# Sparse attention on one core: a deeper ring of steps, two passes over the heads, and top-k selections moved to other places

## The chip, the cores and the metric

The kernel runs on one NeuronCore of a Trainium2 chip. The metric is the device time of one execution in microseconds (us), as the median of several executions. Matrix products run on TensorE (PE in the rows, PEld for its weight loads), the elementwise work on VectorE (DVE) and ScalarE (ACT), some additions on GpSimd (POOL); SyncE (SP) issues the DMAs.

## The reference, cut to what matters

A block of several layers over 528 tokens (16 meta tokens and 512 real ones), of width 1024, all in fp32. The change touches only the sparse attention of the second layer, with 16 heads over a shared latent of rank 256:

```python
def _dsa_attention(h, pos, cid, w_in, latent_norm, w_uq, q_norm, w_uv, rel_bias, k_sel):
    ...
    q_abs, q_idx = jnp.split(c_q @ w_uq, [B_HEADS * B_KV_RANK], axis=-1)
    q_abs = _rms_norm(q_abs.reshape(bsz, t, B_HEADS, B_KV_RANK), q_norm)
    ...
    def block(qa, qi, wi, qpos):
        act = jax.nn.relu(jnp.einsum("bqhd,bsd->bqhs", qi, k_idx) * IDX_DIM ** -0.5)
        score = jnp.einsum("bqh,bqhs->bqs", wi, act).astype(jnp.float32)
        score = jnp.where(cid[None, :] <= cid_q[:, None], score, NEG_INF)
        _, sel = lax.top_k(score, k_sel)            # k_sel = 128
        ...
        logits = (jnp.einsum("bqhr,bqkr->bqhk", qa, kv).astype(jnp.float32) * B_KV_RANK ** -0.5
                  + jnp.swapaxes(bias, -1, -2))
        p = jax.nn.softmax(jnp.where(valid[:, :, None, :], logits, NEG_INF), axis=-1)
        o_lat = jnp.einsum("bqhk,bqkr->bqhr", p.astype(kv.dtype), kv)
        o = jnp.einsum("bqhr,hrd->bqhd", o_lat, w_uv)
```

Each query takes part with the 128 keys of highest index score only. The kernel computes the attention over all keys that a tile of queries can see, and adds a mask of -1e30 where a key is not among the 128.

## The kernel before, in words

Everything stands in `latent_heads`. The 512 queries are cut into four tiles of 128 (`REAL_TILES`); tile t sees 144, 272, 400 or 528 keys. The stage has three parts.

**The query part.** TensorE computes the absorbed queries of the 16 heads (`query`, L1500, four 128x512 products for a head), ScalarE squares them and copies them to `q_all` (L1601, L1603), GpSimd adds the squares and TensorE sums them (`sums`, L1507). Between the queries of heads 0 to 7 stand 40 index jobs, five to a head: a job is one index head of one tile, or half of one for tile 3 (`jobs`; widths 144, 272, 400 and 264). TensorE computes the score (L1516), ScalarE applies the relu (L1591), VectorE adds it into `mb` (L1654, L1657). When a tile's jobs are done, VectorE selects its 128 best keys at once: 16 times `max` and `match_replace` in a loop (L1664 to L1667), each pair taking eight values, then two instructions that turn the row into the mask (L1669, L1671). The engines are tied in a short ring: a relu waits for the addition two jobs back, an index score for the relu three jobs back. So a selection on VectorE holds ScalarE and then TensorE, queries too, since each engine's queue is in order.

**The attention part** runs 64 steps, (head, tile) with the tile running fastest. A step has: two score products on TensorE for each run of up to 512 keys (`scores`, L1535); on VectorE the scaled scores plus bias (L1689) and the mask and row maximum (L1692), together `logit`; on ScalarE the exponentials and their sum (`exps`, L1614); on VectorE the reciprocal of the sum and a diagonal matrix of it (`weigh`, L1698, L1700); on TensorE the transposes of the exponentials against that diagonal (`turn`, L1549); on ScalarE the copy out of the banks (`spread`, L1624, L1628); on TensorE the product with the values (`outputs`, L1559) and on ScalarE its copy (`store`, L1634). The order is written out by hand:

```python
for g in range(LAST):        # TensorE
    turn(g)
    if g + 2 < LAST:
        scores(g + 2)
    if g:
        outputs(g - 1)
for g in range(LAST):        # VectorE
    weigh(g)
    if g + 2 < LAST:
        logit(g + 2)
```

`turn(g)` waits for `weigh(g)`, and `logit(g + 2)` for `scores(g + 2)`. The scores of a step lie in two PSUM banks of their own, of four.

**The output product** (L1580) follows when the last head is stored.

Of the kernel before, what the change touches and what calls it, by code (L numbers as in the profile page):

```python
# [15 lines left out]
P = 128  # L16
# [41 lines left out]
def build(nc, x_t, meta_t, mem_t, bias_onehot, dil_onehot, rel_bias, dil_table, gains, wi, wo, w_out,  # L58
# [3 lines left out]
    with top:  # L62
# [1132 lines left out]
        def dsa_stage():  # L1195
            with ExitStack() as st:
# [8 lines left out]
                early = sb(st, "b_work", [P, 3648])  # L1205
# [225 lines left out]
        def latent_heads(st, qn, ckv, vals, g_lat, kidx, widx, qidx, eps_q, mb, mix, bw, c_bw, early, w_uq, uq_there):  # L1431

            q_all = sb(st, "l_q_all", [P, 2 * B_HEADS, SEQ])
# [4 lines left out]
            nmx = sb(st, "l_nmx", [P, 2])  # L1438
            den = sb(st, "l_den", [P, 2])
            rden = sb(st, "l_rden", [P, 2])  # L1440
# [5 lines left out]
            diag = early[:, 4 * TOK + 10 * P:4 * TOK + 12 * P].rearrange("p (s q) -> p s q", s=2)  # L1446
# [9 lines left out]
            flat = acc[:, :, :].rearrange("p b c -> p (b c)")  # L1456
# [13 lines left out]
            with nc.Block() as block:  # L1470
# [21 lines left out]
                def _(pe):  # L1492
# [36 lines left out]
                    def scores(g):  # L1529
                        hd, t = STEPS_[g]  # L1530
                        _, q0, keys, _ = REAL_TILES[t]
                        for a in range(0, keys, BANK):
                            b = min(keys, a + BANK)
                            for r in range(2):
                                last = pe.matmul(flat[:, 2 * BANK * (g % 2) + a:2 * BANK * (g % 2) + b],  # L1535
                                                 q_all[:, 2 * hd + r, q0 - META:q0 - META + P], ckv[:, r, a:b],
                                                 start=r == 0, stop=r == 1)
                        last.then_inc(scored, 1)

                    def turn(g):  # L1540
                        keys = REAL_TILES[g % NT][2]
# [3 lines left out]
                        for j, n in key_tiles(keys):  # L1545
                            if j == 4 and g >= 2:
                                pe.wait_ge(mixed, 1 + g - 1)
                            to = acc[0:n, 4 + g % 2, j * P:(j + 1) * P] if j < 4 else acc[0:n, 6 + g % 2, P:2 * P]
                            last = pe.matmul(to, e[:, g % 2, j * P:j * P + n], diag[:, g % 2, :], start=True, stop=True)  # L1549
# [14 lines left out]
                    scores(0)  # L1564
                    scores(1)
                    for g in range(LAST):
                        turn(g)
                        if g + 2 < LAST:
                            scores(g + 2)
                        if g:  # L1570
                            outputs(g - 1)
                    outputs(LAST - 1)
                    for c in range(KC):
# [3 lines left out]
                        for k in range(KC):  # L1577
                            if c == 0:
                                pe.wait_ge(mixed, 1 + 2 * NT * (k + 1))
# [5 lines left out]
                def _(act):  # L1585
# [25 lines left out]
                    def exps(g):  # L1611
                        keys = REAL_TILES[g % NT][2]
                        act.wait_ge(logits, 1 + g + 1)
                        act.activation(e[:, g % 2, 0:keys], lg[:, g % 2, 0:keys], ACT.Exp, scale=-1.0,  # L1614
                                       bias=nmx[:, g % 2:g % 2 + 1], accum_out=den[:, g % 2:g % 2 + 1]
                                       ).then_inc(expd, 1)

                    def spread(g):
                        keys = REAL_TILES[g % NT][2]
# [17 lines left out]
                    exps(0)  # L1637
                    exps(1)
                    for g in range(LAST):
# [3 lines left out]
                        if g + 2 < LAST:  # L1643
                            exps(g + 2)
# [3 lines left out]
                def _(dve):  # L1648
                    for n, (i, hd, a, b) in enumerate(jobs):
                        keys = META + (i + 1) * P  # L1650
                        score = mb[:, i, 0:keys]
# [8 lines left out]
                        if hd < IDX_HEADS - 1 or b < keys:  # L1660
                            continue
                        dve.memset(mb[0:CHUNK, i, keys - CHUNK:keys], MASKED)
# [6 lines left out]
                        dve.tensor_scalar(score, score, TAKEN / 1.5, MASKED, ALU.is_gt, ALU.mult)  # L1669
                        dve.drain()  # L1670
                        dve.memset(mb[0:CHUNK, i, keys - CHUNK:keys], MASKED)  # L1671
                        dve.drain()
# [11 lines left out]
                    def logit(g):  # L1684
                        hd, t = STEPS_[g]
                        _, _, keys, y0 = REAL_TILES[t]
                        s = g % 2
# [7 lines left out]
                    def weigh(g):  # L1695
                        s = g % 2
# [5 lines left out]

                    logit(0)
                    logit(1)
                    for g in range(LAST):
                        weigh(g)
                        if g + 2 < LAST:
                            logit(g + 2)
# [1238 lines left out]
```

## Time and profile before

| | us |
|---|---|
| runs | 4040.41, 4052.23, 4040.86 |
| median | 4040.86 |
| the profiled execution's own time | 4044.16 |
| its span in the profile | 4042.5 |
| TensorE busy in the span | 3721.5 (92%) |
| VectorE busy in the span | 1703.9 (42%) |
| query part, first index score to first attention score | 1680.3 to 1841.3 |
| attention part, first score to first output product | 1841.3 to 2122.1 |

A busy TensorE is not TensorE at its peak: the granted clock has two levels, 1.00 (2.4 GHz) and 0.50 (1.2 GHz), and its mean over the span is 0.961. The chain of waits in this profile covers no part of the stage, so the stage is read from its timeline, its waits and its windows.

### The profile page before, as it was taken

To read this page: it belongs to the slowest core of one execution; us is meant where nothing else is said; L and a number is where in the kernel's file an instruction comes from. 1 tells how busy PE (TensorE), PEld (TensorE's weight loads), DVE (VectorE), ACT (ScalarE), POOL (GpSimd) and SP (SyncE) were. 2 spreads that over 40 slices of the span, in tenths; PEclk is the share of its full clock that TensorE was granted. 3 is DMA by queue.
4 is the path that set the end of the run, shared out by engine and by line. 5 is a ranking of instruction groups with operands and counts; after the bars stand their busy time and mean duration, and the time that the engine had idled before them with its cause. 6 is when DMAs were issued, how large, how long until landed. Compare 5 with 4: busy or idle time off the path is not lost. (4 is left out here: it accounts for less than half of the span.)

```text
span 4042.5 us, 51723 instructions
## 1 busy us (share of the span) xinstructions
PE 3721.5 (92%) x20512; PEld 2965.1 (73%) x20512; DVE 1703.9 (42%) x2607; ACT 1277.1 (32%) x1796; POOL 301.0 (7%) x247
## 2 busy tenths in 40 slices
PE   8999798799999998768889999999889899899997
PEld 7999676699999997435555888888634377447886
DVE  4442377344334432253333443443258633225432
ACT  4331466233223321123332432342110143104321
POOL 0000222000000000010000000000045232000000
PEclk9999899799999999879999999999989999999999
DMA  4322311022222223000002222222212231223221
GB/s 166 131 77 79 112 53 48 32 94 88 80 99 89 90 79 126 8 21 16 1 1 94 93 94 93 104 93 88 99 39 78 89 96 53 101 75 114 94 85 71
DMA packets 115307, 318.04 MB, mean 79 GB/s; under 512 B 13335, under 2 KB 56471, under 8 KB 99060
## 3 DMA queue, kind: packets, MB, share of 16 engines
q1 hardware_dynamic: 115188, 316.48, 22.8%
q8 instruction: 71, 1.16, 0.1%
q14 instruction: 48, 0.39, 0.0%
HBM read 307.95 MB, written 17.01 MB: 80 GB/s over the span
## 5 line engine op out<-in xcount | busy, mean ns | idle before, releaser
L326 PE MATMUL acc<-fb_xh,fb_wh 128*128 128x264 f32 x1408 | 287.9, 286 | 11.7 <-DVE fb_wl L476 11.7
L326 PE MATMUL acc<-fb_xl,fb_wh 128*128 128x264 f32 x1408 | 288.3, 286 | 0.0
L326 PE MATMUL acc<-fb_xh,fb_wl 128*128 128x264 f32 x1408 | 287.7, 286 | 0.0
L326 PE MATMUL acc<-fd_xh,fd_wh 128*128 128x512 f32 x704 | 275.4, 391 | 9.6 <-DVE fd_wl L476 9.6
L326 PE MATMUL acc<-fd_xl,fd_wh 128*128 128x512 f32 x704 | 274.4, 390 | 0.0
L326 PE MATMUL acc<-fd_xh,fd_wl 128*128 128x512 f32 x704 | 274.4, 390 | 0.0
L326 PEld LDWEIGHTS acc<-fb_xh,fb_wh 128*128 128x128 f32 x1408 | 220.1, 189 | 12.1 <-DVE fb_wl L476 11.9
L326 PEld LDWEIGHTS acc<-fb_xl,fb_wh 128*128 128x128 f32 x1408 | 219.4, 189 | 0.0
L326 PEld LDWEIGHTS acc<-fb_xh,fb_wl 128*128 128x128 f32 x1408 | 219.1, 189 | 0.0
L397 ACT ACTIVATE fb_wh<-fb_raw 128x2048 fp32r<-128x2048 f32 (+1 forms) x74 | 124.7, 1685 | 290.1 <-PE acc L385 177.0
L471 DVE TENSOR_TENSOR fb_wl<-fb_raw,fb_wh 128x2048 fp32r<-128x2048 f32 (+1 forms) x74 | 148.3, 2004 | 141.4 <-ACT fb_wh L397 140.5
L471 DVE TENSOR_TENSOR fd_wl<-fd_raw,fd_wh 128x2048 fp32r<-128x2048 f32 (+1 forms) x74 | 148.3, 2003 | 136.5 <-ACT fd_wh L397 135.5
L397 ACT ACTIVATE fd_wh<-fd_raw 128x2048 fp32r<-128x2048 f32 (+1 forms) x74 | 124.8, 1686 | 255.8 <-PE acc L385 162.4
L397 ACT ACT_TABLE_LOAD x60 | 77.0, 1283 | 301.2 <-PE acc L326 301.1
L1874 PE MATMUL acc<-m_xn,s_gw 128*128 128x512 f32 x384 | 171.5, 603 | 0.0
L326 PEld LDWEIGHTS acc<-fd_xh,fd_wh 128*128 128x128 f32 x704 | 132.5, 188 | 38.5 <-DVE fd_wl L476 10.7
L326 PE MATMUL acc<-fa_xh,fa_wh 128*128 128x264 f32 x704 | 144.3, 286 | 11.9 <-DVE fa_wl L476 11.9
L326 PEld LDWEIGHTS acc<-fd_xl,fd_wh 128*128 128x128 f32 x704 | 132.5, 188 | 27.9 <-issue 0.5
L326 PEld LDWEIGHTS acc<-fd_xh,fd_wl 128*128 128x128 f32 x704 | 132.4, 188 | 27.5
L326 PE MATMUL acc<-ff_xh,ff_wh 128*128 128x512 f32 x352 | 138.2, 393 | 8.0 <-DVE ff_wl L476 8.0
L1874 PEld LDWEIGHTS acc<-m_xn,s_gw 128*128 128x128 f32 x384 | 72.7, 192 | 98.2 <-issue 98.2
L326 PE MATMUL acc<-fa_xl,fa_wh 128*128 128x264 f32 x704 | 144.5, 287 | 0.0
(523 smaller groups left out, 8472.2 us busy)
## 6 DMA issues: line engine op xcount, KB each, us to landing
fb_raw<-wi_dram SPq DMA_DIRECT2D x42, 1024.0 KB, 4.7
fd_raw<-wi_dram SPq DMA_DIRECT2D x42, 1024.0 KB, 4.7
fb_raw<-wo_dram SPq DMA_DIRECT2D x32, 704.0 KB, 3.9
fd_raw<-wo_dram SPq DMA_DIRECT2D x32, 704.0 KB, 4.0
fa_raw<-wi_dram SPq DMA_DIRECT2D x20, 1024.0 KB, 4.7
ff_raw<-wi_dram SPq DMA_DIRECT2D x20, 1024.0 KB, 4.7
a_raw<-a_qkv_dram SPq DMA_DIRECT2D x24, 512.0 KB, 4.0
s_gw<-gate_w_dram SPq DMA_DIRECT2D x24, 512.0 KB, 3.9
```

The source lines that it names most:

```text
L326: last = pe.matmul(acc[:, up_base(p, b) + 2 * a + q, 0:w], x[:, k, a, :], part[:, k, t0:t0 + w], start=k == 0 and part is xh and x is wv, ...
L397: act.activation(wh[:, b, 0:n_], raw[:, b, 0:n_], ACT.Copy).then_inc(rounded, 1)
L471: dve.tensor_tensor(wl[:, b, 0:n_], raw[:, b, 0:n_], wh[:, b, 0:n_].bitcast(F32), ALU.subtract).then_inc(split, 1)
L1874: last = pe.matmul(acc[:, GATE_BANK[n % 2], :], gw[:, n % 3, k * P:(k + 1) * P], xn[:, k, :], start=k == 0, stop=k == KC - 1)
```

## The change

What it does:

- The steps run in two passes over the heads: first tiles 0 and 1 of all 16 heads, then tiles 2 and 3.
- Four steps are in flight in place of two (`DEEP`), each with one score bank, and `scores`, `logit` and `exps` run three steps ahead (`AHEAD`). The last 16 keys of tile 3 don't fit into its bank; their scores are computed with those of tile 2, in whose bank they find room, and VectorE reads them by an instruction of its own. The exponentials are written over the logits.
- The selection of tile 0 is spread between the index jobs of tiles 1 to 3: one `pick` (a `max` and a `match_replace`) after every second job. Those of tiles 1 and 2 come in one piece each after the last job. That of tile 3 moves into the first pass: one `pick` after the `logit` at tile 1 of heads 0 to 13, two at heads 6 and 13.

```diff
+            DEEP, AHEAD = 4, 3
...
-            lg = early[:, 0:2 * TOK].rearrange("p (s t) -> p s t", s=2)
-            e = early[:, 2 * TOK:4 * TOK].rearrange("p (s t) -> p s t", s=2)
+            lg = early[:, 0:4 * TOK].rearrange("p (s t) -> p s t", s=DEEP)
...
-            STEPS_ = [(hd, t) for hd in range(B_HEADS) for t in range(NT)]
+            STEPS_ = [(hd, t) for first in (0, 2) for hd in range(B_HEADS) for t in (first, first + 1)]
+            REST_AT = REAL_TILES[NT - 2][2]
...
                     def scores(g):
                         hd, t = STEPS_[g]
-                        for a in range(0, keys, BANK):
-                            b = min(keys, a + BANK)
+                        if g >= DEEP:
+                            pe.wait_ge(logits, 1 + g - DEEP + (2 if t == NT - 2 else 1))
+
+                        def part(to, t_, a, b):
+                            q0 = REAL_TILES[t_][1] - META
                             for r in range(2):
-                                last = pe.matmul(flat[:, 2 * BANK * (g % 2) + a:2 * BANK * (g % 2) + b],
-                                                 q_all[:, 2 * hd + r, q0 - META:q0 - META + P], ckv[:, r, a:b],
-                                                 start=r == 0, stop=r == 1)
+                                last = pe.matmul(acc[:, g % DEEP, to:to + b - a], q_all[:, 2 * hd + r, q0:q0 + P],
+                                                 ckv[:, r, a:b], start=r == 0, stop=r == 1)
+                            return last
+
+                        last = part(0, t, 0, min(REAL_TILES[t][2], BANK))
+                        if t == NT - 2:
+                            last = part(REST_AT, NT - 1, BANK, TOK)
                         last.then_inc(scored, 1)
...
-                    scores(0)
-                    scores(1)
+                    for g in range(AHEAD):
+                        scores(g)
                     for g in range(LAST):
                         turn(g)
-                        if g + 2 < LAST:
-                            scores(g + 2)
+                        if g + AHEAD < LAST:
+                            scores(g + AHEAD)
                         if g:
                             outputs(g - 1)
...
+                    def pick(i):
+                        score = mb[:, i, 0:META + (i + 1) * P]
+                        dve.max(top8[:, :], score)
+                        dve.drain()
+                        dve.match_replace(out=score, in_to_replace=top8[:, :], in_values=score, imm_value=TAKEN)
+                        dve.drain()
...
                     for n, (i, hd, a, b) in enumerate(jobs):
...
-                        with dve.Fori(0, TOPK // 8):
-                            dve.max(top8[:, :], score)
-                            dve.drain()
-                            dve.match_replace(out=score, in_to_replace=top8[:, :], in_values=score, imm_value=TAKEN)
-                            dve.drain()
...
+                        done = n + 1 - IDX_HEADS
+                        if done > 0:
+                            rest = len(jobs) - IDX_HEADS
+                            for _ in range(done * PICKS // rest - (done - 1) * PICKS // rest):
+                                pick(0)
+                    visible(0)
+                    for i in (1, 2):
+                        with dve.Fori(0, PICKS):
+                            pick(i)
+                        visible(i)
...
                     def logit(g):
...
-                        dve.scalar_tensor_tensor(lg[:, s, 0:keys], flat[:, 2 * BANK * s:2 * BANK * s + keys],
-                                                 rq[:, t, hd:hd + 1], bw[:, hd, y0:y0 + keys], ALU.mult, ALU.add)
+                        own = min(keys, BANK)
+                        dve.scalar_tensor_tensor(lg[:, s, 0:own], acc[:, s, 0:own], rq[:, t, hd:hd + 1],
+                                                 bw[:, hd, y0:y0 + own], ALU.mult, ALU.add)
+                        if keys > BANK:
+                            dve.scalar_tensor_tensor(lg[:, s, BANK:keys], acc[:, s - 1, REST_AT:REST_AT + keys - BANK],
+                                                     rq[:, t, hd:hd + 1], bw[:, hd, y0 + BANK:y0 + keys],
+                                                     ALU.mult, ALU.add)
...
+                    LATE, LAST_PICK = NT - 1, B_HEADS - 3
                     for g in range(LAST):
+                        hd, t = STEPS_[g]
                         weigh(g)
-                        if g + 2 < LAST:
-                            logit(g + 2)
+                        if g + AHEAD < LAST:
+                            logit(g + AHEAD)
+                        if t == 1 and hd <= LAST_PICK:
+                            for _ in range((hd + 1) * PICKS // (LAST_PICK + 1) - hd * PICKS // (LAST_PICK + 1)):
+                                pick(LATE)
+                            if hd == LAST_PICK:
+                                visible(LATE)
```

`exps`, `turn` and `weigh` follow with `g % DEEP`, and `PICKS` is 16.

How this moves instructions, on VectorE first. In the query part, around the end of the jobs of tile 0 (`b_mb` holds the index scores and later the mask, `b_work` the relus), before:

```order
L1657 SCALAR_TENSOR_TENSOR b_mb<-b_work,b_widx,b_mb 128x144 x7
L1662 MEMSET b_mb 64x64
L1664 UNCONDITIONAL_BRANCH
L1665 MAX l_top<-b_mb 128x8
L1667 MATCH_REPLACE b_mb<-l_top,b_mb 128x144
L1664 REGISTER_ALU
L1664 COMPARE_AND_BRANCH
L1669 TENSOR_SCALAR b_mb<-b_mb 128x144
L1671 MEMSET b_mb 64x64
L1654 TENSOR_SCALAR b_mb<-b_work,b_widx 128x272
```

and in the changed kernel:

```order
L1681 SCALAR_TENSOR_TENSOR b_mb<-b_work,b_widx,b_mb 128x144 x7
L1685 MEMSET b_mb 64x64
L1678 TENSOR_SCALAR b_mb<-b_work,b_widx 128x272
L1681 SCALAR_TENSOR_TENSOR b_mb<-b_work,b_widx,b_mb 128x272
L1661 MAX l_top<-b_mb 128x8
L1663 MATCH_REPLACE b_mb<-l_top,b_mb 128x144
L1681 SCALAR_TENSOR_TENSOR b_mb<-b_work,b_widx,b_mb 128x272 x2
L1661 MAX l_top<-b_mb 128x8
L1663 MATCH_REPLACE b_mb<-l_top,b_mb 128x144
```

The loop of 16 rounds that stood ahead of the next tile's jobs is gone from there; its rounds stand one by one between those jobs.

In the attention part, VectorE over one step and a half, before (in `b_work` lie the logits and the diagonals here; the row ISA is the mask and maximum):

```order
L1689 SCALAR_TENSOR_TENSOR b_work<-acc,l_rq,b_bw 128x144
L1692 ISA b_work,l_nmx<-b_work,b_mb 128x144
L1692 ISA l_nmx 128x1
L1698 RECIPROCAL l_rden<-l_den 128x1
L1700 TENSOR_SCALAR b_work<-ident,l_rden 128x128
L1689 SCALAR_TENSOR_TENSOR b_work<-acc,l_rq,b_bw 128x272
```

and in the first pass of the changed kernel:

```order
L1714 SCALAR_TENSOR_TENSOR b_work<-acc,l_rq,b_bw 128x144
L1721 ISA b_work,l_nmx<-b_work,b_mb 128x144
L1721 ISA l_nmx 128x1
L1661 MAX l_top<-b_mb 128x8
L1663 MATCH_REPLACE b_mb<-l_top,b_mb 128x528
L1727 RECIPROCAL l_rden<-l_den 128x1
L1729 TENSOR_SCALAR b_work<-ident,l_rden 128x128
L1714 SCALAR_TENSOR_TENSOR b_work<-acc,l_rq,b_bw 128x272
```

A `pick` of tile 3, 528 wide, has come between a `logit` and the `weigh` that follows it; that `weigh` is of the step two before the `logit`'s, where it was one before.

In the second pass on VectorE:

```order
L1714 SCALAR_TENSOR_TENSOR b_work<-acc,l_rq,b_bw 128x512
L1717 SCALAR_TENSOR_TENSOR b_work<-acc,l_rq,b_bw 128x16
L1721 ISA b_work,l_nmx<-b_work,b_mb 128x528
L1721 ISA l_nmx 128x1
L1727 RECIPROCAL l_rden<-l_den 128x1
L1729 TENSOR_SCALAR b_work<-ident,l_rden 128x128
```

The row of 528 that stood at L1689 for tile 3 is now two rows, of 512 and 16.

## Rows read from the trace of the kernel before

**Rows 1.** Windows: us, then busy us of each engine, granted clock, DMA share, GB/s.

```profile
1680.30:1841.30 161.00, 104.92 (x336) 54.87 (x337) 90.71 (x244) 48.72 (x88) 20.33 (x16) 0.77 0.07 22
1855.30:2122.10 266.80, 223.91 (x1193) 140.08 (x1191) 89.08 (x307) 91.71 (x309) 0.00 (x0) 1.00 0.00 1
```

**Rows 2.** Waits over the query part: engine and line, waited for, us, times, longest.

```profile
PE acc L1516 <- ACT b_work L1591: 54.2, 7, 22.2
```

**Rows 3.** Timeline of the query part, TensorE and VectorE: start, us, operation, [idle before].

```profile
1700.31 0.72 PE L1516 MATMUL acc<-b_work 64*128 64x272 f32 x2
...
1721.30 0.11 DVE L1662 MEMSET b_mb<- 64x64 f32 x1
...
1743.84 0.43 DVE L1654 TENSOR_SCALAR b_mb<-b_work,b_widx 128x400 f32<-128x400 f32 x1
...
1755.81 0.11 DVE L1662 MEMSET b_mb<- 64x64 f32 x1
...
1782.68 0.81 DVE L1654 TENSOR_SCALAR b_mb<-b_work,b_widx 128x264 f32<-128x264 f32 x2
...
1794.81 1.15 PE L1516 MATMUL acc<-b_work 64*128 64x264 f32 x6
...
1801.98 1.16 PE L1516 MATMUL acc<-b_work 64*128 64x264 f32 x6
...
1806.37 0.11 DVE L1662 MEMSET b_mb<- 64x64 f32 x1
```

**Rows 4.** Timeline of VectorE, last selection, and the first logit.

```profile
1833.15 0.71 DVE L1665 MAX8 l_top<-b_mb 128x8 f32<-128x528 f32 x1 [0.34 <-issue]
...
1834.01 0.69 DVE L1667 MATCH_REPLACE8 b_mb<-l_top,b_mb 128x528 f32<-128x528 f32 x1
...
1841.49 0.23 DVE L1675 SCALAR_TENSOR_TENSOR l_mean_u<-acc,b_eps_q 128x64 f32<-128x64 f32 x1 [4.00 <-PE acc L1507]
...
1842.74 0.37 DVE L1689 SCALAR_TENSOR_TENSOR b_work<-acc,l_rq,b_bw 128x144 f32<-128x144 f32 x1
```

**Rows 5.** Timeline of TensorE over one head of the attention part.

```profile
1949.47 1.18 PE L1535 MATMUL acc<-b_ckv,l_q_all 128*128 128x272 f32 x4
...
1952.26 0.81 PE L1549 MATMUL acc<-b_work 128*128 128x128 f32 x4 [0.44 <-DVE b_work L1700]
1953.00 1.61 PE L1535 MATMUL acc<-b_ckv,l_q_all 128*128 128x400 f32 x4
...
1956.47 1.03 PE L1549 MATMUL acc<-b_work 128*128 128x128 f32 x6 [0.49 <-DVE b_work L1700]
1957.43 2.33 PE L1535 MATMUL acc<-b_ckv,l_q_all 128*128 128x512 f32 x8
...
1961.90 1.26 PE L1549 MATMUL acc<-b_work 128*128 128x128 f32 x8 [1.41 <-DVE b_work L1700]
1963.09 0.76 PE L1535 MATMUL acc<-b_ckv,l_q_all 128*128 128x144 f32 x4
...
1965.18 1.48 PE L1549 MATMUL acc<-b_work 128*128 128x128 f32 x10 [0.39 <-DVE b_work L1700]
```

**Rows 6.** Timeline of VectorE, a logit of the same head.

```profile
1963.88 0.37 DVE L1689 SCALAR_TENSOR_TENSOR b_work<-acc,l_rq,b_bw 128x144 f32<-128x144 f32 x1 [2.04 <-PE acc L1535]
```

**Rows 7.** Groups of instructions, VectorE at 16 elements out of PSUM: busy, mean ns, idle before.

```profile
L1063 DVE CUSTOM_DVE_ANT_0 a_lg<-acc,a_bw 128x16 f32<-128x16 f32 x16 | 2.1, 168 | 0.0
```

**Rows 8.** Timeline of TensorE at the half clock, start of the attention part.

```profile
1845.77 1.33 PE L1549 MATMUL acc<-b_work 128*128 128x128 f32 x4 [1.60 <-DVE b_work L1700]
1847.03 3.04 PE L1535 MATMUL acc<-b_ckv,l_q_all 128*128 128x400 f32 x4
```

**Rows 9.** Windows in two other stages (columns as in rows 1).

```profile
440.00:455.80 15.80, 8.40 (x31) 7.20 (x32) 9.44 (x12) 7.91 (x12) 7.60 (x6) 0.50 0.33 109
3439.00:3442.40 3.40, 3.40 (x10) 2.68 (x9) 0.36 (x1) 0.94 (x1) 0.00 (x0) 0.51 0.00 0
```

**Rows 10.** Timeline of TensorE ahead of the second of these windows.

```profile
3437.78 1.09 PE L2376 MATMUL acc<-ident,d_xe 128*128 128x128 f32 x8 [2.31 <-DVE d_xe L2642]
```

More of the change, by code:

```diff
@@ L1548, in turn @@
                             to = acc[0:n, 4 + g % 2, j * P:(j + 1) * P] if j < 4 else acc[0:n, 6 + g % 2, P:2 * P]
-                            last = pe.matmul(to, e[:, g % 2, j * P:j * P + n], diag[:, g % 2, :], start=True, stop=True)
+                            last = pe.matmul(to, lg[:, g % DEEP, j * P:j * P + n], diag[:, g % DEEP, :],
+                                             start=True, stop=True)
                         last.then_inc(turned, 1)
@@ L1635, in store @@
                                        acc[0:64, 6 + g % 2, 0:P], ACT.Copy).then_inc(mixed, 1)
-                    exps(0)
-                    exps(1)
+                    for g in range(AHEAD):
+                        exps(g)
                     for g in range(LAST):
@@ L1648, in _, with visible @@
                 def _(dve):
+                    PICKS = TOPK // 8
+                    def pick(i):
[4 more added lines that the diff above has]
+                        dve.drain()
+                    def visible(i):
+                        keys = META + (i + 1) * P
+                        dve.tensor_scalar(mb[:, i, 0:keys], mb[:, i, 0:keys], TAKEN / 1.5, MASKED, ALU.is_gt, ALU.mult)
+                        dve.drain()
+                        dve.memset(mb[0:CHUNK, i, keys - CHUNK:keys], MASKED)
+                        dve.drain()
                     for n, (i, hd, a, b) in enumerate(jobs):
                         keys = META + (i + 1) * P
-                        score = mb[:, i, 0:keys]
                         dve.wait_ge(relued, 1 + n + 1)
@@ L1659, in _ @@
                         dve.drain()
-                        if hd < IDX_HEADS - 1 or b < keys:
-                            continue
-                        dve.memset(mb[0:CHUNK, i, keys - CHUNK:keys], MASKED)
-                        dve.drain()
-                        with dve.Fori(0, TOPK // 8):
-                            dve.max(top8[:, :], score)
-                            dve.drain()
-                            dve.match_replace(out=score, in_to_replace=top8[:, :], in_values=score, imm_value=TAKEN)
-                            dve.drain()
[L1669 to L1672, printed above, removed]
+                        if hd == IDX_HEADS - 1 and b == keys:
+                            dve.memset(mb[0:CHUNK, i, keys - CHUNK:keys], MASKED)
+                            dve.drain()
+                        done = n + 1 - IDX_HEADS
[8 more added lines that the diff above has]
+                        visible(i)
                     dve.wait_ge(ssq_mm, 1 + B_HEADS)
@@ L1701, in weigh @@
                                           ALU.mult).then_inc(weights, 1)
-                    logit(0)
-                    logit(1)
+                    for g in range(AHEAD):
+                        logit(g)
+                    LATE, LAST_PICK = NT - 1, B_HEADS - 3
                     for g in range(LAST):
+                        hd, t = STEPS_[g]
                         weigh(g)
-                        if g + 2 < LAST:
-                            logit(g + 2)
+                        if g + AHEAD < LAST:
+                            logit(g + AHEAD)
[4 more added lines that the diff above has]
+                                visible(LATE)
                     for c in range(KC):
```

32 lines of the change are left out of this document (15 added, 17 removed).

## The prediction

> **What bounds the kernel now.** No chain of waits crosses the stage, so I read it from windows, waits and timelines. The windows [rows 1] part it in two. In the query part TensorE is busy for 104.9 of 161 us at a mean clock of 0.77; in the attention part for 224 of 267 us at 1.00. The reader should see that the first part idles and runs slow, the second hardly idles.
>
> In the query part TensorE's longest waits are at the index scores, 54.2 us in seven waits, the longest 22.2 [rows 2]. They stand where VectorE selects: 22.5 us between the memset at 1721.30 and the next tile's work at 1743.84, and 26.9 us from 1755.81 to 1782.68 [rows 3]. Where nothing is selected, a head with five jobs takes 7.17 us (1794.81 to 1801.98) [rows 3]. So VectorE's selections bound this part, by way of the in-order queues.
>
> In the attention part every `turn` is preceded by an idle time that a `weigh` ends: 0.44, 0.49, 1.41 and 0.39 us in a head, 2.73 together [rows 5]. VectorE in turn begins a `logit` right behind the scores, after waiting 2.04 us for them [rows 6]. That is a closed chain: turn(g), scores(g+2), logit(g+2), weigh(g+1), turn(g+1). `outputs` lies inside the VectorE leg and is hidden in all four steps.
>
> **Query part, step by step.** Both kernels do the same up to 1700.31, the end of the third query; the first selection had just begun. From there the new kernel has five more queries with jobs. At 7.17 us each that is 35.9, and the jobs of 400 keys add some 0.4 to each of two heads: 36.7, so the eighth query ends at about 1737.0. A `pick` of tile 0 is short, and two or three in a head fit beside the additions into 7.17 us, so I cost them at nothing; their cover is the query on TensorE. Behind the last query with jobs VectorE took 4.4 us before (1801.98 to 1806.37) [rows 3]; with two picks of tile 0 and the mask I take 6.8, to 1743.8. Then tiles 1 and 2 in one piece, 22.5 + 26.9 less 0.4 for the memsets that stand elsewhere: 49.0, to 1792.8. TensorE has the last eight queries beside this and is done some 17 us earlier, so its terms cost nothing. The first logit followed 1.25 us after L1675 [rows 4]; now at 1794.1, before at 1842.74. **Gain: 48.6 us.** Of this 31 is the selection of tile 3, which only moves; the rest is the stalls of tiles 0 to 2 at the full and half clock.
>
> **Attention part: does the depth remove a wait?** With three steps ahead the order is turn(g), scores(g+3), outputs(g-1) on TensorE and weigh(g), logit(g+3), weigh(g+1) on VectorE. `weigh(g+1)` still stands behind `logit(g+3)`, this behind `scores(g+3)`, and these behind `turn(g)`. The chain is the old one with another index. What becomes looser is the exponential, which was never waited for there. So I put the depth at zero. The order of tiles matters little too: every step is turn + scores + VectorE's leg, and each occurs as often as before. In pass one a pair of steps takes T0 0.74 (1952.26 to 1953.00), S1 with its leg 2.79 (1949.47 to 1952.26), T1 0.96 (1956.47 to 1957.43) and S0 with its leg 2.09 (1963.09 to 1965.18): 6.58 us [rows 5].
>
> - The picks of tile 3 stand between `logit(g+3)` and `weigh(g+1)`, on the chain, at steps where nothing else waits; no cover is left once `outputs` of 0.7 us is done. One is 0.86 from the start of MAX8 to that of MATCH_REPLACE8, 0.69 for the latter, and some 0.12 for the drain: 1.67 [rows 4] (the 0.34 "issue" is the loop's, which is gone). Sixteen are 26.7, the mask 0.8: **+27.5**.
> - Splitting the 528-wide logit adds an instruction of 16 elements from PSUM, on the chain sixteen times. The nearest row has 168 ns for such a one [rows 7]: **+2.7**.
> - The scores of the last 16 keys move from one step to its neighbour: 0. VectorE does three logits before the first `weigh` in place of two: **+0.6**. The new waits of `scores` are for logits three or four steps old: 0.
>
> At an unchanged clock this is +30.8, and the sum -17.8.
>
> **The clock.** Pass one gives TensorE less to do. A pair with a pick lasts 6.58 + 1.67 = 8.25 us, of which some 5.2 are busy, with an idle gap of about 2.4. It begins after 17 us of idleness, so at 0.50. Two rows speak of such a load. Between 440 and 456 TensorE worked in bursts, 8.4 of 15.8 us, and stayed at 0.50 all the time [rows 9]. At 3437.78 it came out of a gap of 2.31 us with short products only [rows 10], and the clock was 0.51 behind it, from 1.00 [rows 9]. In the attention part before the idle gaps were at most 1.41 and the clock held 1.00 [rows 1, 5]. So I expect pass one to run mostly at 1.2 GHz. Its price: T0 took 1.26 us there (1845.77 to 1847.03) against 0.74, a factor of 1.7 [rows 5, 8]; the products themselves can at most double. On T0 + T1 + S0 + S1 (0.74, 0.96, 0.76, 1.18) that is 2.5 to 3.0 us a pair, if VectorE's leg stays; in sixteen pairs 40 to 48. Before, the attention part paid about 4 for its own slow start, so 36 to 44, or 40, if the whole pass is slow. Since at the half clock a pair is one busy run of some 9 us, it may recover here and there; I take five sixths, **+33**. The bounds are 0 and +44.
>
> The Trainium skill (TensorE: Matmul & The Clock Gate, in the section Why this matters for your kernels) lays the drop of the clock to idle gaps longer than those worked out here. By that rule pass one would warm up and stay warm, and the sum would be -18. The trace speaks against it, since 2.31 us were enough at 3437.78; it stays as a rival below.
>
> **The sum:** -48.6 + 30.8 + 33 = +15, so 4059 against the profiled execution's own 4044.16. That execution lies 3.3 us above the median of the runs; **for the median I predict 4056 us.** A measurement of this kernel tells 0.3%, 12 us, from no change.
>
> **Rivals.**
>
> 1. *The clock recovers in about half of pass one.* For it: the unbroken runs of 9 us at the half clock. The term is 20 in place of 33: +2, 4043.
> 2. *The full clock through pass one*, as by the page's rule: -18, 4023. For it: 60% busy, no gap over 2.4. Against it: rows 9 and 10. This one ends on the faster side; it decides where the clock term is under 6.
> 3. *The jobs don't run freely.* The picks of tile 0 delay the additions, these the relus, and by the ring of three the queries, so that only the moved selection's 31 us come off: -31 + 31 + 33 = +33, 4074. For it: this ring made the stalls of rows 2. Against it: five additions and 2.5 picks need some 5.5 us of the 7.17.
> 4. *The depth does what it says*: VectorE runs ahead, the picks and the idle 2.73 us of a head are hidden. Then -48.6 - 44 + 3 = -90, 3951. Against it: the order above. The change not doing what it says is thus my forecast.
>
> **Chances.** Forecast 0.54, of which 0.18 falls within 12 us of no change and 0.36 above; its own range is 4047 to 4066. Rival 1 0.20, all within. Rival 2 0.14, 0.11 faster and 0.03 within. Rival 3 0.08, slower. Rival 4 0.04, faster. Faster 0.15, same 0.41, slower 0.44. The range takes in rival 2 at its lower end and all but the last of rival 3: 4023 to 4073; about 0.15 is left outside.
>
> **What would show it.** Right: first logit near 1794; TensorE without a long wait at the index scores; in pass one a pair of turns every 8 to 11 us, with a wait for L1729 of 2 us or more after each pick, and a granted clock near 0.5 over most of it; in pass two a wait ahead of each `turn` as before. Wrong: turns in pass one without these waits (rival 4), a clock of 1.00 there (rival 2), or index scores that wait for VectorE in the query part (rival 3).

## The result, and the profile after

| | before | changed kernel |
|---|---|---|
| median, us | 4046.14 (16 runs, 4040.41 to 4052.4) | 4053.46 (16 runs, 4047.74 to 4060.15) |
| the profiled execution, us | 4044.16 | 4050.23 |
| its span, mean granted clock | 4042.5, 0.961 | 4048.5, 0.956 |
| TensorE busy, us | 3721.5 | 3741.5 |
| VectorE busy, us | 1703.9 | 1709.2 |
| query part: first index score to L1675 / L1699 (`l_mean_u`), us | 161.2 | 117.1 |
| attention part: from there to the first output product, us | 280.6 | 332.3 |
| sum of both parts, us | 441.8 | 449.4 |

The ratio is 1.0018 with a 95% interval of 1.0010 to 1.0025: 7 us slower, less than the 0.3% that I called no change. The stage explains all of it: -44.1 us in its first part, +51.7 in its second, +7.6 together, where the two profiled executions are 6.1 us apart.

The windows of the changed kernel over the same stretches; the first answers to the query window of [rows 1], the other two are the first and the second pass, from the first `weigh` of a pass to the next pass, or to the last `weigh` (us, then busy us of each engine, granted clock, DMA share, GB/s):

```profile
1681.30:1798.40 117.10, 97.48 (x348) 53.08 (x348) 67.32 (x194) 48.76 (x88) 20.25 (x16) 0.89 0.12 39
...
1802.06:1964.65 162.59, 122.48 (x450) 71.05 (x450) 63.84 (x214) 40.57 (x160) 0.00 (x0) 0.72 0.00 1
1964.65:2121.98 157.33, 133.14 (x693) 83.71 (x694) 52.50 (x166) 50.56 (x147) 0.00 (x0) 0.99 0.00 1
```

The waits of the changed kernel in the stage, the engine and line, what it waited for, us, times, longest:

```profile
DVE b_work L1714 <- PE acc L1537: 189.1, 61, 5.2
PE acc L1555 <- DVE b_work L1729: 81.5, 52, 17.9
```

The same two waits in the kernel before:

```profile
DVE b_work L1689 <- PE acc L1535: 168.4, 63, 4.9
PE acc L1549 <- DVE b_work L1700: 46.4, 63, 1.9
```

The first says that VectorE still stands before nearly every `logit` waiting for the scores. The second says that TensorE still waits for `weigh` at most of the `turn`s. Four steps in flight have freed neither engine. Of the 54.2 us at the index scores [rows 2] 4.1 us are left, in six waits, the longest 1.8.

The query part, TensorE and VectorE (start, us, operation, [idle before]). It answers to [rows 3] and [rows 4]:

```profile
1721.72 3.70 PE L1500 MATMUL acc<-b_cq,b_w_uq 128*128 128x512 f32 x8
...
1729.06 5.40 PE L1500 MATMUL acc<-b_cq,b_w_uq 128*128 128x512 f32 x8
...
1737.92 3.70 PE L1500 MATMUL acc<-b_cq,b_w_uq 128*128 128x512 f32 x8
1741.55 1.16 PE L1516 MATMUL acc<-b_work 64*128 64x264 f32 x6
...
1748.58 0.45 DVE L1661 MAX8 l_top<-b_mb 128x8 f32<-128x272 f32 x1
...
1798.21 0.11 DVE L1671 MEMSET b_mb<- 64x64 f32 x1
...
1799.65 0.37 DVE L1714 SCALAR_TENSOR_TENSOR b_work<-acc,l_rq,b_bw 128x144 f32<-128x144 f32 x1
```

The eighth query ends at 1741.55, against the predicted 1737.0. One query of eight products took 5.40 us instead of 3.70, where the clock had fallen for a moment (the granted clock over the query is 0.68); the one at 1712.63 took 5.40 too. These two are 3.4 of the 4.5 us, and 0.9 is that the whole stage began that much later in this execution. The selections of tiles 1 and 2 then take 49.6 us (1748.58 to 1798.21; predicted 49.0).

A step with a pick in the first pass, at the full clock up to the turn and partly at the half clock behind it; it answers to [rows 5] and [rows 6]:

```profile
1879.28 0.37 DVE L1714 SCALAR_TENSOR_TENSOR b_work<-acc,l_rq,b_bw 128x144 f32<-128x144 f32 x1 [1.81 <-PE acc L1537]
...
1880.00 0.71 DVE L1661 MAX8 l_top<-b_mb 128x8 f32<-128x528 f32 x1
1880.78 0.09 DVE L1663 MATCH_VALUE_LOAD b_mb<-l_top,b_mb 128x8 f32 x1
1880.85 0.69 DVE L1663 MATCH_REPLACE8 b_mb<-l_top,b_mb 128x528 f32<-128x528 f32 x1
1881.62 0.16 DVE L1727 RECIPROCAL l_rden<-l_den 128x1 f32<-128x1 f32 x1
1881.86 0.28 DVE L1729 TENSOR_SCALAR b_work<-ident,l_rden 128x128 f32<-128x128 f32 x1
1882.20 0.81 PE L1555 MATMUL acc<-b_work 128*128 128x128 f32 x4 [2.24 <-DVE b_work L1729]
1882.94 1.70 PE L1537 MATMUL acc<-b_ckv,l_q_all 128*128 128x272 f32 x4
```

The chain of the prediction stands in these lines: scores, `logit`, the pick (1.62 us from 1880.00 to 1881.62), `weigh`, `turn`, with TensorE idle for 2.24 us at the end. At the two heads with two picks the gap is longer; the prediction, with "no gap over 2.4", had overlooked these. The first of them:

```profile
1872.79 1.02 PE L1555 MATMUL acc<-b_work 128*128 128x128 f32 x4 [3.87 <-DVE b_work L1729]
```

The clock can be read from the pairs of steps. Two such turns at the half clock, then two at the full clock:

```profile
1850.40 1.33 PE L1555 MATMUL acc<-b_work 128*128 128x128 f32 x4 [1.73 <-DVE b_work L1729]
...
1861.43 1.34 PE L1555 MATMUL acc<-b_work 128*128 128x128 f32 x4 [1.73 <-DVE b_work L1729]
...
1901.94 0.81 PE L1555 MATMUL acc<-b_work 128*128 128x128 f32 x4 [2.24 <-DVE b_work L1729]
...
1910.38 1.03 PE L1555 MATMUL acc<-b_work 128*128 128x128 f32 x4 [2.47 <-DVE b_work L1729]
```

11.03 us against 8.44: the half clock costs 2.6 us a pair, or 2.8 against the pair of 8.20 from 1823.40 to 1831.60, whose gaps are both 2.24; 2.5 to 3.0 were worked out. But the mean clock of the pass is 0.72, so it was at the lower level for 0.56 of the time (1 - 0.56 / 2 = 0.72), not for the five sixths that I took. Its first 16 us, from the first turn at 1802.64 on, are among that: TensorE had stood for 17.9 us ahead of it, as the selections of tiles 1 and 2 on VectorE end later than the last query.

### The profile page after: what moved, and what is told of

It reads as the page before. It is cut to its first block and busy times, and to the rows that moved or that the text cites. A ratio compares the mean times of both kernels' runs of the same rounds, so it can differ in the third digit from the quotient of the medians.

```text
span 4048.5 us, 51673 instructions
## 1 busy us (share of the span) xinstructions
PE 3741.5 (92%) x20512; PEld 2978.5 (74%) x20512; DVE 1709.2 (42%) x2623; ACT 1277.8 (32%) x1796; POOL 300.6 (7%) x247
## 5 line engine op out<-in xcount | busy, mean ns | idle before, releaser
L397 ACT ACTIVATE fd_wh<-fd_raw 128x2048 fp32r<-128x2048 f32 (+1 forms) x74 | 124.8, 1686 | 255.8 <-PE acc L385 162.4
L1555 PE MATMUL acc<-b_work 128*128 128x128 f32 (+1 forms) x448 | 82.6, 316 | 81.6 <-DVE b_work L1729 81.5
```

Of the source, the lines that this page charges most:

```text
L397: act.activation(wh[:, b, 0:n_], raw[:, b, 0:n_], ACT.Copy).then_inc(rounded, 1)
L1555: last = pe.matmul(to, lg[:, g % DEEP, j * P:j * P + n], diag[:, g % DEEP, :], start=True, stop=True)
```

## The experiments

The theory, in short: the attention part is a closed chain in which `weigh(g+1)` stands on VectorE behind `logit` of a later step; the depth does nothing because of that; the moved picks lengthen the chain by 1.6 us each; and with the idle gaps that they make the clock is lower. The rivals: the depth is worth or costs something by itself, the picks or the clock cost nothing, or another part of the change (order of tiles, split logit) makes the loss.

### One part of the change alone

**b3_attention_part**: the kernel before with the new attention part (four steps in flight, two passes, split logit), without any picks in it, and with the old query part. As a difference from the changed kernel:

```diff
-                        done = n + 1 - IDX_HEADS
-                        if done > 0:
-                            rest = len(jobs) - IDX_HEADS
-                            for _ in range(done * PICKS // rest - (done - 1) * PICKS // rest):
-                                pick(0)
-                    visible(0)
-                    for i in (1, 2):
-                        with dve.Fori(0, PICKS):
-                            pick(i)
-                        visible(i)
+                            with dve.Fori(0, PICKS):
+                                pick(i)
+                            visible(i)
...
-                        if t == 1 and hd <= LAST_PICK:
-                            for _ in range((hd + 1) * PICKS // (LAST_PICK + 1) - hd * PICKS // (LAST_PICK + 1)):
-                                pick(LATE)
-                            if hd == LAST_PICK:
-                                visible(LATE)
```

> The changed kernel with the query part of the kernel before (each tile selected at once behind its jobs), so the attention part alone: two passes, four steps in flight, the logit of 528 in two instructions, no picks in it. Theory (depth and order are worth nothing, the split 2.7 us and the start 0.6): 3 us more than before at an equal clock, 4047 to 4055 us. Rival 1 (the depth hides part of the wait ahead of turn): 4035 us or less. Rival 2 (the half clock comes of the short steps of the first pass, picks or not): 4060 us or more.

Measured: 4047.76 us, ratio 0.9998 (0.9989 to 1.0007). Its first pass and its wait ahead of the turns:

```profile
1847.64:1959.88 112.24, 89.83 (x450) 53.91 (x450) 39.55 (x162) 40.47 (x160) 0.00 (x0) 0.97 0.00 1
```

```profile
PE acc L1555 <- DVE b_work L1722: 48.2, 61, 1.6
```

The time is that of the kernel before, and inside the range expected. The depth, the passes and the split together cost 2.9 us in the attention part (283.5, before 280.6), about the 3.3 forecast for the split and the start; the wait ahead of the turns is 48.2 us, where it was 46.4. Against this kernel the changed one has 48.8 us more in its attention part (332.3 and 283.5). The picks are the only difference in the code there. Sixteen at 1.62 and the mask make 26.7. The remaining 22 I put down to the clock: the first pass ran at 0.97 without the picks, at 0.72 with them, though TensorE does the same work. They are a remainder, not a measurement, and hold the slow start behind the 17.9 us as well, which comes of the new query part and which this run doesn't have. A second estimate, from 0.56 of the pass in pairs of 11.03 us that each cost 2.6 to 2.8 more, gives 21 to 23.

**b2_query_part**: the kernel before with only the new query part, in which all four selections stay.

```diff
-                        if hd < IDX_HEADS - 1 or b < keys:
-                            continue
...
+                        done = n + 1 - IDX_HEADS
+                        if done > 0:
+                            rest = len(jobs) - IDX_HEADS
+                            for _ in range(done * PICKS // rest - (done - 1) * PICKS // rest):
+                                pick(0)
+                    visible(0)
+                    for i in (1, 2, 3):
+                        with dve.Fori(0, PICKS):
+                            pick(i)
+                        visible(i)
```

> The kernel before with only the query part changed: picks of tile 0 between the jobs, the selections of tiles 1, 2 and 3 in one piece behind the last job; the attention part as before. Theory (freeing the jobs is worth the stalls of TensorE, apart from the selection that moves): in the changed kernel the first logit came 118 us behind the first index score, and tile 3's selection adds 31, so 149.5 in place of 162.4: 13 us less, 4033 us, at most 4038. Rival (VectorE's total work sets the query part and only moving work away shortens it): 4046 us, no change.

Measured: 4036.91 us, ratio 0.9975 (0.9964 to 0.9987), within the expectation. The query part takes 150.8 us, 10.4 less than before and 33.7 more than in the changed kernel. These two can't be taken as they stand, since in this execution the clock was low for longer at the start of the part. The third query, here and in the changed kernel:

```profile
1697.38 3.70 PE L1500 MATMUL acc<-b_cq,b_w_uq 128*128 128x512 f32 x8
...
1697.60 3.70 PE L1500 MATMUL acc<-b_cq,b_w_uq 128*128 128x512 f32 x8
```

It begins 19.0 us behind the first index score (1678.39) here and 16.3 behind it (1681.26) there; before it was 16.4. The two queries ahead of it took 6.46 and 4.95 us here, 5.40 and 3.70 there. Without these 2.7 us the part is 148.1. So of the 44 us 31 are the last tile's selection, which only moves, as predicted, and 13 are the stalls, where the prediction had 17.6.

### The order on VectorE

**a1_pick_early**: the changed kernel with the pick ahead of the `logit`, where VectorE waits for the scores.

```diff
                         weigh(g)
-                        if g + AHEAD < LAST:
-                            logit(g + AHEAD)
                         if t == 1 and hd <= LAST_PICK:
...
+                        if g + AHEAD < LAST:
+                            logit(g + AHEAD)
```

> The changed kernel with each pick of tile 3 moved from behind logit(g+3) to ahead of it, that is into the time in which VectorE waits for the scores. Theory (the picks cost because they stand on the chain scores, logit, weigh, turn): VectorE waits 2 to 3.5 us there and a pick takes 1.67, so the 27 us of picks go, and with the shorter gaps on TensorE part of the half clock too, 10 to 21 us: 4006 to 4017 us. Rival (VectorE's work in the first pass is too much wherever it stands): 4045 us or more, no change by over 8.

Measured: 4018.92 us, ratio 0.9919 (0.9903 to 0.9936), 2 us above what the theory gave and far from the rival; the attention part takes 297.1 us, 35 less than in the changed kernel. From its timeline:

```profile
1873.22 0.70 DVE L1661 MAX8 l_top<-b_mb 128x8 f32<-128x528 f32 x1
...
1874.07 0.69 DVE L1663 MATCH_REPLACE8 b_mb<-l_top,b_mb 128x528 f32<-128x528 f32 x1
...
1875.12 0.37 DVE L1714 SCALAR_TENSOR_TENSOR b_work<-acc,l_rq,b_bw 128x144 f32<-128x144 f32 x1 [0.35 <-PE acc L1537]
...
1876.41 0.81 PE L1555 MATMUL acc<-b_work 128*128 128x128 f32 x4 [0.61 <-DVE b_work L1729]
```

The same pick now lies in VectorE's wait, which shrinks to 0.35 us, and TensorE's gap ahead of the turn is 0.61 in place of 2.24. A pair takes 6.57 us (1869.84 to 1876.41), which is the 6.58 that the prediction worked out for a pair without a pick, and 1.63 less than the 8.20 of a pair with one at the full clock. The clock of the pass is 0.84. Of the 35 us 26.7 are the picks and some 8 the clock, a little less than the 10 to 21 expected for it. So the picks cost what they cost by their place in the queue.

**a2_weigh_first**: the changed kernel with `weigh(g+1)` ahead of `logit(g+3)`.

```diff
-                        weigh(g)
+                        if g == 0:
+                            weigh(0)
+                        if g + 1 < LAST:
+                            weigh(g + 1)
                         if g + AHEAD < LAST:
                             logit(g + AHEAD)
```

> The changed kernel with weigh(g+1) ahead of logit(g+3) on VectorE, the picks left behind the logit. Theory (the depth does nothing because weigh(g+1) is queued behind logit(g+3), which needs scores(g+3)): the chain now has a whole step of slack, TensorE no longer waits ahead of turn (some 44 us), the picks are hidden (27 us) and the clock is held (some 20): near 3960 us, TensorE's wait for the diagonal under 10 us in total. Rival (ScalarE's copies, or the score banks, close a chain of the same length): 4010 us or more.

Measured: 3960.93 us, ratio 0.9783 (0.9767 to 0.9800). Its two passes:

```profile
1801.63:1895.80 94.17, 90.71 (x438) 55.74 (x438) 61.41 (x209) 38.44 (x155) 0.00 (x0) 0.89 0.00 1
1895.80:2029.05 133.25, 133.25 (x714) 85.17 (x712) 53.68 (x170) 51.89 (x152) 0.00 (x0) 1.00 0.00 1
```

In the second pass TensorE is busy for all of the 133.25 us; in the changed kernel it was busy for 133.14 of 157.33. The wait for `weigh`, 52 times in the changed kernel, is left three times. It is 20.8 us in all, not under 10 as expected, since 17.9 of them stand ahead of the first turn, where TensorE waits for the end of the query part on VectorE.

**b1_weigh_first**: the same swap in the kernel before, two steps deep, with nothing else of the change.

```diff
-                        weigh(g)
+                        if g == 0:
+                            weigh(0)
+                        if g + 1 < LAST:
+                            weigh(g + 1)
                         if g + 2 < LAST:
                             logit(g + 2)
```

> The kernel before, two steps in flight as it was, with weigh(g+1) ahead of logit(g+2). Theory (the order on VectorE set the wait, not the depth): the exponential of step g+1 is ready while TensorE still has outputs, turn and scores to do, so nearly all of the 44 us of idle time ahead of turn goes: 4002 us, at most 4012. Rival (four steps in flight are needed for this order, since weigh(g+1) now follows logit(g+1) directly and waits for its exponential): 4035 us or more.

Measured: 3993.61 us, ratio 0.9864 (0.9848 to 0.9880), 8 us better than the 4002 expected. Its windows over the 64 steps, in two halves, and its waits:

```profile
1843.80:1955.60 111.80, 111.26 (x584) 70.60 (x584) 47.38 (x159) 44.70 (x156) 0.00 (x0) 0.97 0.01 2
1955.60:2066.50 110.90, 110.90 (x598) 70.18 (x597) 47.40 (x155) 44.56 (x156) 0.00 (x0) 1.00 0.00 1
```

```profile
DVE b_work L1689 <- PE acc L1535: 62.5, 48, 3.6
DVE l_rden L1698 <- ACT b_work L1614: 53.7, 63, 1.1
```

VectorE now waits for the exponentials (53.7 us, where it was 0.5 us once), and it costs nothing: TensorE is busy throughout. The chain that made the wait of [rows 5] was thus one of order, and changing the place of one call takes it out at a depth of two.

**a6_weigh_first_ahead2**: a2_weigh_first with `AHEAD` 2 in place of 3.

```diff
-            DEEP, AHEAD = 4, 3
+            DEEP, AHEAD = 4, 2
```

> The changed kernel with weigh(g+1) ahead of logit, and AHEAD 2 in place of 3. Whether depth is worth something once the order is right. If not: 3955 to 3968 us, as with AHEAD 3 (3961). If it is: weigh(g+1) now follows logit(g+1) and the pick directly and must wait for an exponential, and in the first pass a logit, a pick and a weigh (3.2 us) fill the slack of one step: 3972 us or more.

Measured: 3962.80 us, ratio 0.9792 (0.9778 to 0.9805), 2 us from a2_weigh_first. Once the order is right TensorE is the bound (busy for all of the 143 us from 1900 to 2043 here), and the third step ahead has nothing left to hide.

### The clock

**a3_filler**: the changed kernel with products that nothing uses: sixteen of 512 columns ahead of the first turn, and two behind the outputs of every pair in the first pass.

```diff
                         scores(g)
+                    for _ in range(16):
+                        pe.matmul(acc[:, 4, :], ident[:, :], q_all[:, 0, :], start=True, stop=True)
...
+                        if g and g < 2 * B_HEADS and STEPS_[g][1] == 1:
+                            for _ in range(2):
+                                pe.matmul(acc[:, 4 + (g + 1) % 2, :], ident[:, :], q_all[:, 0, :], start=True, stop=True)
```

> The changed kernel with products added that nothing uses: sixteen of 512 columns while TensorE waits for the first diagonal, and two of 512 columns after outputs at every odd step of the first pass, where the picks leave TensorE idle for 2.4 us. Theory (some 20 us of the first pass are the half clock, which comes of the idle gaps): granted clock near 1.00 over the first pass, and 4030 to 4036 us. Rival (the time is that of the chain alone and the clock costs little): 4053 us or more, since the added products can only lengthen it.

Measured: 4034.85 us, ratio 0.9970 (0.9957 to 0.9982). Its first pass:

```profile
1801.77:1946.19 144.42, 123.99 (x512) 67.36 (x513) 63.81 (x212) 40.59 (x160) 0.00 (x0) 0.93 0.00 1
```

More work on TensorE, and the pass is 18.2 us shorter. The time is as expected; the clock is 0.93, not near 1.00. So the clock cost at least 18 us, and the 22 of b3_attention_part fit.

**a4_ahead2**: the changed kernel with `AHEAD` 2 (the same line as in a6_weigh_first_ahead2).

> The changed kernel with AHEAD 2 in place of 3, everything else the same. Theory (weigh stands behind logit at any depth): within 6 us of the changed kernel, 4047 to 4059 us. Rival (the third step in flight hides something, the exponential or ScalarE's copies): 4065 us or more.

Measured: 4064.40 us, ratio 1.0047 (1.0033 to 1.0060), 11 us above the changed kernel. That is 5 us above what the theory allowed and 0.6 below where the rival begins, so the theory missed here. Its first pass:

```profile
1798.96:1973.51 174.55, 133.70 (x446) 78.97 (x446) 63.22 (x212) 40.54 (x159) 0.00 (x0) 0.64 0.00 1
```

It is 12 us longer than with `AHEAD` 3, and the clock is 0.64 in place of 0.72. **a7_ahead2_filler** puts the products of a3_filler into it, to see which of the two it is:

> The changed kernel with logits one step less far ahead (as in a4_ahead2) and with the unused 512-column products of a3_filler in the first pass. a4_ahead2 came out 11 us above the changed kernel, at a granted clock of 0.64 in the first pass instead of 0.72. Theory: depth itself is worth nothing while the weighing stands behind the next logit on VectorE, and those 11 us are TensorE's lower clock; with the products that keep it higher the clock goes back to about 0.9 and the time to that of a3_filler (4034.9), within 6 us: 4030 to 4041. Rival: the third step in flight does hide something of its own, whatever the clock; then the 11 us stay on top of a3_filler: 4045 us or more.

Measured: 4037.54 us, ratio 0.9983 (0.9974 to 0.9992).

```profile
1800.88:1950.00 149.12, 129.31 (x509) 70.05 (x510) 63.25 (x212) 40.75 (x159) 0.00 (x0) 0.89 0.00 1
```

The time lies in the theory's range, not in the rival's. With the clock held at 0.89 the 11 us shrink to 3 by the medians, 5 by the ratios. Most of what looks like a gain by the third step ahead is clock. A little is its own: at the half clock a pair takes 11.28 us in a4_ahead2 (1885.60 to 1896.88) and 11.03 in the changed kernel. Why the clock falls more often at `AHEAD` 2 isn't settled; other scores follow the gap there (144 keys wide, where it was 272), and nothing tried here takes that apart.

### A version faster than both

**c1_more_picks_late**: a2_weigh_first, in which ten of the sixteen picks of the third tile stand in the first pass too, one pick at each of the first 26 steps.

```diff
-                    for i in (1, 2):
-                        with dve.Fori(0, PICKS):
-                            pick(i)
-                        visible(i)
+                    KEPT = 6
+                    with dve.Fori(0, PICKS):
+                        pick(1)
+                    visible(1)
+                    with dve.Fori(0, KEPT):
+                        pick(2)
...
+                    MORE = [3 if n % 2 or n >= 20 else 2 for n in range(26)]
+                    MORE_2 = [n for n in range(26) if MORE[n] == 2]
...
+                        if g < len(MORE):
+                            pick(MORE[g])
+                            if g in (MORE_2[-1], len(MORE) - 1):
+                                visible(MORE[g])
```

> a2_weigh_first (3960.9 us) with ten of the sixteen picks of the third tile taken out of the query part as well and put into the first pass, one pick at each of its first 26 steps (ten of the third tile, sixteen of the last). Theory: with the weighing ahead of the next logit TensorE is what the pairs of the first pass wait for, and a pick on VectorE fits beside it, so the query part loses ten times 1.62 us and little comes back: 3943 to 3952 us, the first logit 16 us earlier. Rival: with a pick at every step VectorE has 6.0 us of work per pair against 5.2 us on TensorE and becomes the bound of the first pass, and gives the gain back: 3958 us or more.

Measured: 3939.91 us, ratio 0.9741 (0.9727 to 0.9754), 105 us faster than before and the fastest of all, and 3 us below the lower end of what the theory gave. Its first pass, the last work on TensorE ahead of it, and two turns:

```profile
1785.18:1876.16 90.98, 82.99 (x438) 51.00 (x438) 72.84 (x243) 37.29 (x155) 0.00 (x0) 1.00 0.00 1
```

```profile
1779.55 1.05 PE L1507 MATMUL acc<-ones,l_late 128*128 128x1 f32 x8 [1.67 <-POOL l_late L1488]
1780.47 3.82 PE L1537 MATMUL acc<-b_ckv,l_q_all 128*128 128x144 f32 x12
...
1829.89 0.81 PE L1555 MATMUL acc<-b_work 128*128 128x128 f32 x4 [0.32 <-DVE b_work L1731]
...
1835.44 0.81 PE L1555 MATMUL acc<-b_work 128*128 128x128 f32 x4 [0.32 <-DVE b_work L1731]
```

VectorE is busy for 72.84 of 90.98 us in it, 11 more than in a2_weigh_first, and the pass is still 3.2 us shorter. TensorE comes from its last query straight into the scores, without the wait of 17.9 us; the query part is 17.0 us shorter than in a2_weigh_first. And the clock is 1.00 over the pass, not 0.89. The rival's mechanism did come in part, for TensorE waits for `weigh` 16 times again. A pair takes 5.55 us, where it takes 5.17 at the full clock in a2_weigh_first (1834.67 to 1839.84). That is some 5 us over thirteen pairs, which uses up most of the clock's gain, but leaves that of the query part.

## Why the prediction was right, and where it wasn't

The time was right: 4056 us forecast, 4053.46 measured. That it is so close is luck. The forecast was the 4040.86 us known then and 15 more; the difference measured is +6 on the profiled executions and +7.3 by the medians, for the kernel before has a median of 4046.14 over sixteen runs. Nor was no change what I held likeliest: the forecast stood just outside the 12 us, and the chances were slower 0.44, same 0.41. The mechanism was right, but two terms were too large, and their errors partly cancel.

- **Depth at zero, tiles' order at zero: right.** b3_attention_part has both and the time of the kernel before. The reason is shown as well: `weigh` put ahead of `logit`, at either depth, frees what the depth didn't. Under the picks the third step ahead is worth a little, 3 to 5 us by a7_ahead2_filler.
- **Picks, +27.5: right.** 1.62 us each against 1.67, so 26.7 with the mask. a1_pick_early shows that they cost by their place alone.
- **Split logit, +2.7: about right.** From the start of the `logit` to the mask it was 0.88 us before (1959.81 to 1960.69), now 1.01 (L1714 at 2044.70, L1721 at 2045.71): 0.13 for each of sixteen, 2.1 together. The 16-wide instruction itself takes 0.23, more than the 0.168 of [rows 7]; why only 0.13 of it shows isn't settled.
- **Query part, -48.6: mis-sized, measured -44.0** to the first logit (162.4 to 118.4 us behind the first index score). The step that failed is "At 7.17 us each that is 35.9": it took the full clock for all five heads, and in two the clock fell during the query, 1.7 us each. The other 1.2 are spread; among them, the last jobs to the mask took 7.0 us, not 6.8, and the two selections 49.6, not 49.0.
- **Clock, +33: mis-sized, measured about 22.** The step that failed is "I take five sixths". The price for a pair was right (2.6 to 2.8 us), the share of the pass was not: 0.56. With 40 us for the whole pass that is 22.4, and by b3_attention_part 22. In this the case came out as rival 1, "the clock recovers in about half of pass one", with a term of 20. By it the sum is +2; with the 4.6 us that the query part lacks it is +7, what was measured. So in mechanism and in the difference (+2 against +15, measured +7) the rival was nearer than the forecast, and only the median as a number favours the forecast.
- **Rival 2, the full clock, fell**: behind the gaps of 2.47 us at 1910.38 and 2.24 us at 1919.80 the clock drops from 1.00 to 0.50. By the rule of the Trainium skill (TensorE: Matmul & The Clock Gate, Why this matters for your kernels), which lays the drop to longer idle gaps than these, the pass would have stayed warm at the steps with one pick. The trace disagrees.
- **Rival 3 fell**: in the query part TensorE waits for an index relu for 4.1 us in all, where it was 54.2. **Rival 4 fell** for this kernel, but its time, 3951, is near that of a2_weigh_first (3961), where the order lets the depth's promise come true, mostly without the depth.

The reading of the order that put the depth at zero could have been carried one step further: the swap of `weigh` and `logit`, worth 53 us even in the kernel before, is in the same five instructions.

## What to carry to other kernels

Before an in-order pipeline is made deeper, write down for each engine what stands ahead of the instruction that the bound engine waits for. If it is work for a later step that itself waits for the bound engine, more depth only changes an index, and putting the earlier step's work first is what frees the chain. Work moved out of a serial part costs its full length behind such an instruction and little or nothing in the wait ahead of it, and the clock can nearly double its price (here 27 us of picks, and some 22 us of clock, the slow start of the pass included).

## What the runs showed of the hardware

- In the first pass of the changed kernel six gaps of 2.24 us stand ahead of a turn with the clock at 1.00. Behind four of them it fell to 0.50 (the turns at 1831.60, 1840.81, 1882.20 and 1919.80), behind two it didn't (1823.40 and 1901.94). It fell behind the gaps of 2.47 (1910.38) and 3.87 us (1872.79) too. In a1_pick_early it held 1.00 behind one of 1.96 (1856.68), in a3_filler it fell behind one of the same length (1865.80).
- A gap of such a length isn't needed. In a2_weigh_first the clock fell at about 1845.5, and the only gap near it is this one of 1.07 us:

```profile
1843.77 1.03 PE L1555 MATMUL acc<-b_work 128*128 128x128 f32 x6 [1.07 <-DVE b_work L1729]
```

  In the query part of the changed kernel it fell at about 1713 and 1729.9, where TensorE hadn't waited for over 0.6 us since 1700. So no length of a gap found here tells the share of a pass at the half clock beforehand. That the picks' gaps lower the clock rests on the means of the pass: 0.72 with them, 0.84 with the picks moved (a1_pick_early), 0.93 with the gaps filled (a3_filler), 0.97 without picks (b3_attention_part).
- The half clock cost 2.6 to 2.8 us on a pair of steps of 8.2 to 8.4, not twice the time, since VectorE's part of the chain stays as it is.
- The same selection, moved off the query part, was worth nothing where the picks stand on the chain (31 us saved, 49 spent). Where they don't, most of the gain is kept: from b1_weigh_first to a2_weigh_first, both with `weigh` first, the query part is 44 us shorter (selection and stalls), and the time falls by 33.
